# Bias column of the layer norm on Pool, and a reordered gMLP step, in a two-layer hybrid decoder trunk

## The reference, cut to what matters

```python
h = x * (1 + sc) + sh
x = layer_norm(DEEPNORM_ALPHA * x + (1 + gt) * y, g, b)   # y = mixer or MoE of h

z = gelu(h @ w_in + b_in); u, v = split(z)                # the gMLP, u and v of width 2048
v = layer_norm(v, sgu_ln_g, sgu_ln_b)
mixed = einsum('gts,bnsgc->bntgc', tril(w_s), v) + b_s    # over 128 tokens of a chunk, 8 groups
y = (u * mixed) @ w_out + b_out
```

## Time and profile before

| | us |
|---|---|
| median of 3 runs | 2381.33 (2380.76 to 2382.56) |
| the profiled execution, its own time | 2371.53 |
| its span, slowest core (core 3) | 2370.5 |
| spans of the eight cores | 2345.4 to 2370.5 |
| PE busy / DVE / ACT / POOL in the span | 1320.1 / 1281.0 / 618.6 / 447.9 |

### The profile page before, as it was taken

One profiled execution on the slowest core, in us unless ns is written; L12 is line 12 of the kernel. 1 busy time (PEld: TensorE's weight loads), 2 busy tenths in 40 slices (PEclk: granted clock), 3 DMA queues, 4 the chain that ended last, 5 costly groups with the idle time before them and its releaser, 6 DMA issues.

```text
span 2370.5 us, 30701 instructions; the slowest of 8 cores (2345.4 to 2370.5 us)
## 1 busy us (share of the span) xinstructions
PE 1320.1 (56%) x9655; PEld 808.7 (34%) x9655; DVE 1281.0 (54%) x2578; ACT 618.6 (26%) x1191; POOL 447.9 (19%) x562
## 2 busy tenths in 40 slices
PE   1657667675074444553327988888843555556300
PEld 0334334443053333342114444434422433334200
DVE  2465555654354444461338667676644545555488
ACT  1435335342021111121113434434321211112000
POOL 1030020112221111110112221313113111111252
PEclk9778889887587777776668999999976877778655
DMA  9958847489889999999854888668695999999752
GB/s 167 185 115 98 108 73 115 81 97 120 129 157 241 235 220 198 251 217 218 231 123 75 165 160 160 136 140 151 103 192 171 214 255 243 251 258 257 278 197 97
DMA packets 91387, 407.91 MB, mean 172 GB/s; under 512 B 20261, under 2 KB 20261, under 8 KB 79525
## 3 DMA queue, kind: packets, MB, share of 16 engines
q0 software_dynamic: 41584, 211.43, 56.5%
q1 hardware_dynamic: 49626, 194.34, 24.0%
HBM read 449.24 MB, written 160.53 MB: 257 GB/s over the span
## 4 chain that ended last, share of the span: by engine, by line
DMA 34%; PE 23%; DVE 22%; issue 11%; another core or an unknown queue 4%; ACT 3%; POOL 2%; DVEq 1%; SPq 1%; ACTq 0%; POOLq 0%
DMA sb_W<-wb 7%; DMA sb_x<-xd 6%; PE bank L1384 5%; DMA ys<-sb_Z 3%; DMA sb_A<-adaP 3%; DMA sb_W<-ys,sb_idx 3%; PE bank L1076 3%; PE bank L1704 3%; DMA ys<-sb_hT 2%; PE bank L917 2%; DVE sb_x L1450 2%; DMA sb_W<-moe_w 2%; PE bank L1630 2%; DMA xd<-sb_hT 2%
## 5 line engine op out<-in xcount | busy, mean ns | idle before, releaser
L1384 PE MATMUL bank<-sb_hT,sb_W 128*128 128x256 bf16 x1984 | 308.0, 322 | 185.8 <-DMA sb_W<-wb 164.4
L1384 PEld LDWEIGHTS bank<-sb_hT,sb_W 128*128 128x128 bf16 x1984 | 222.2, 115 | 240.8 <-issue 188.3
L1366 ACT ACTIVATE sb_hT<-bank,sb_H 128x256 bf16<-128x256 f32 x256 | 130.1, 561 | 441.5 <-PE bank L1357 433.0
L1371 DVE TENSOR_SCALAR sb_hT<-bank,sb_H 128x256 bf16<-128x256 f32 x256 | 126.8, 537 | 183.3 <-PE bank L1357 147.8
L1409 DVE TENSOR_TENSOR sb_hT<-bank,sb_gtbf 128x512 f32<-128x512 f32 x176 | 121.4, 691 | 76.4 <-DMA ys<-sb_hT 59.8
L1704 PE MATMUL bank<-sb_W,sb_Z 128*128 128x512 bf16 x512 | 137.6, 417 | 14.9 <-ACT sb_Z L1697 14.9
L610 POOL TENSOR_TENSOR sb_rstdt<-sb_mvt,sb_eps_t 128x1 f32<-128x1 f32 x64 | 25.8, 404 | 586.4 <-DVE sb_R L448 247.9
L1630 PE MATMUL bank<-sb_x,sb_Z 128*128 128x512 bf16 x512 | 127.4, 393 | 11.6 <-DVE sb_cact_rep L1685 5.6
L1405 PE MATMUL bank<-sb_W,sb_R 128*128 128x512 bf16 x496 | 130.8, 410 | 1.2 <-DVE sb_hT L1409 1.2
L1661 PE MATMUL bank<-sb_x,sb_Z 128*128 128x512 bf16 x512 | 123.5, 383 | 5.8 <-issue 5.8
L1346 POOL DMA_INDIRECT sb_hT<-xh,sb_slots x64 | 60.9, 951 | 330.6 <-PE bank L1357 286.5
(11 more groups left out here) (260 smaller groups left out, 2696.4 us busy)
## 6 DMA issues: line engine op xcount, KB each, us to landing
wb<-moe_w POOLq DMA_DIRECT2D x38, 1536.0 KB, 16.6
sb_W<-wb SPq DMA_DIRECT2D x36, 1536.0 KB
ys<-sb_hT SPq DMA_DIRECT2D x44, 1024.0 KB
sb_W<-moe_w POOLq DMA_DIRECT2D x26, 1536.0 KB, 21.1
ys<-sb_Z SPq DMA_DIRECT2D x20, 1024.0 KB
sb_A<-adaP POOLq DMA_DIRECT2D x30, 512.0 KB, 14.6
sb_x<-xin SPq DMA_DIRECT2D x16, 512.0 KB, 9.7
xd<-sb_x SPq DMA_DIRECT2D x16, 512.0 KB, 47.0
```

The source lines that it names most:

```text
L1366: S.op("act", (lambda k=k, src=src: lambda e: e.activation(out=hTe[i][:, k, :], in_=src, func=AF.Identity, scale=H1[haff][:, k:k + 1], bia ...
L1371: S.op("dve", (lambda k=k, src=src: lambda e: e.tensor_scalar(out=hTe[i][:, k, :], in0=src, scalar1=H1[haff][:, k:k + 1], scalar2=H0[haff] ...
L1384: S.op("pe", (lambda k=k, f=f, fc=fc: lambda e: e.matmul(banks[bk][:, f * 256:(f + 1) * 256], wgu[:, k, fc:fc + 128], hTe[i][:, k, :], sta ...
```

## The change

1. `ln_stats` now also makes the column -mean x rstd, by two Pool instructions behind `rsqrt` (one multiplies the mean by a constant -1, one multiplies that by rstd), in a column for each tile. The DVE instruction L620 of `ln_xhat` goes.
2. In the gMLP the bn_stats of v leaves `gV` and is issued one step later (`gVs(i+3)`), behind `gU`.
3. The four mean subtractions of a tile are issued one in each step of that tile, ahead of `gB`. bn_aggr and `rsqrt` of v go from cb = 3 of the tile before to cb = 0 of the tile.
4. For the returned tile, `ln_stats`, `ln_xhat` and `finalize_b` go one step later each: from cb = 3, 0, 1 to cb = 0, 1, 2. `tl_combine`, `tl_fetch` and `affine` stay in their steps.

```diff
-        mvt = sb("mvt", [128, NT, 2]); rstdt = sb("rstdt", [128, NT]); nmr_ = [sb(f"nmr{i}", [128, 1]) for i in range(2)]
+        mvt = sb("mvt", [128, NT, 2]); rstdt = sb("rstdt", [128, NT]); nmrt = sb("nmrt", [128, NT])
...
+        S.op("dve", lambda e: e.memset(mone[:], -1.0), writes=[Beps])
...
             rsqrt(rstdt[:, t:t + 1], Brstd_[t], mvt[:, t, 1:2], Bmv_[t])
+            nm = nmrt[:, t:t + 1]
+            S.op("pool", lambda e: e.tensor_tensor(out=nm, in0=mvt[:, t, 0:1], in1=mone[:], op=ALU.mult),
+                 reads=[Bmv_[t], Beps], writes=[Bnmr_[t]])
+            S.op("pool", lambda e: e.tensor_tensor(out=nm, in0=nm, in1=rstdt[:, t:t + 1], op=ALU.mult),
+                 reads=[Brstd_[t], Bnmr_[t]], writes=[Bnmr_[t]])
...
-            S.op("dve", lambda e: e.scalar_tensor_tensor(out=nmr[:], in0=mvt[:, t, 0:1], scalar=-1.0,
-                                                         in1=rstdt[:, t:t + 1], op0=ALU.mult, op1=ALU.mult),
-                 reads=[Bmv_[t], Brstd_[t]], writes=[Bnmr])
-            S.op("act", lambda e: e.activation(out=dst, in_=xa, func=AF.Identity, scale=rstdt[:, t:t + 1], bias=nmr[:]),
-                 reads=[bxa, Brstd_[t], Bnmr], writes=[bdst])
+            S.op("act", lambda e: e.activation(out=dst, in_=xa, func=AF.Identity, scale=rstdt[:, t:t + 1],
+                                               bias=nmrt[:, t:t + 1]),
+                 reads=[bxa, Brstd_[t], Bnmr_[t]], writes=[bdst])
...
             S.op("act", lambda e: e.activation(out=v, in_=banks[bk][:], func=AF.Gelu), reads=[PB[bk]], writes=[bv])
-            S.op("dve", lambda e: e.bn_stats(out=gst[:, i2, cb, :], in_=v), reads=[bv], writes=[Bgst[i2]])
-
-        def v_norm(t, part):
+
+        def gVs(j):
+            t, cb = divmod(j, 4)
             i2 = t % 2
-            if part == 0:
+            S.op("dve", lambda e: e.bn_stats(out=gst[:, i2, cb, :], in_=v32[j % NV]), reads=[Bv32[j % NV]], writes=[Bgst[i2]])
+
+        def v_norm(t, cb):
+            i2 = t % 2
+            if cb == 0:
                 S.op("dve", lambda e: e.bn_aggr(out=mvg[:, i2, :], in_=gst[:, i2, :, :]),
                      reads=[Bgst[i2]], writes=[Bmvg[i2]])
                 rsqrt(rstdg[:, i2:i2 + 1], Brstdg[i2], mvg[:, i2, 1:2], Bmvg[i2])
-            for cb in ((0, 1, 2), (3,))[part]:
...
                 gU(i)
+            if 0 <= i + 3 < 4 * NT:
+                gVs(i + 3)
+            if 0 <= i < 4 * NT:
+                v_norm(t, cb)
             if 1 <= i <= 4 * NT:
                 gB(i - 1)
             if cb == 0 and 0 <= t < NT:
                 ws_scale(t)
-                v_norm(t, 1)
...
-            if cb == 3 and 0 <= t + 1 < NT:
-                v_norm(t + 1, 0)
...
             if cb == 3 and 0 <= t + 3 < NT:
                 tl_combine(t + 3)
-                ln_stats(t + 3)
...
             if 0 <= t + 2 < NT:
                 if cb == 0:
+                    ln_stats(t + 2)
+                if cb == 1:
                     ln_xhat(t + 2, xnb[0], Bxnb[0])
-                if cb == 1:
+                if cb == 2:
                     finalize_b(t + 2, 0, 2, hdst=hTg[(t + 2) % 3], bhdst=BhTg[(t + 2) % 3], on_act=8)
-                if cb == 2:
                     affine(t + 2)
```

More of the change, by code:

```diff
@@ L314, in build @@
         Badfm, BadabT, Bmod = [Buf(f"adfm{j}") for j in range(6)], Buf("adabT"), [Buf(f"mod{i}") for i in range(4)]
-        Bnmr_ = [Buf(f"nmr{i}") for i in range(2)]
+        Bnmr_ = [Buf(f"nmr{t}") for t in range(NT)]; mone = sb("mone", [128, 1])
         fin_i = [0]
@@ L617, in ln_xhat @@
             xa, bxa = xv[t]
-            i = fin_i[0] % 2
-            nmr, Bnmr = nmr_[i], Bnmr_[i]
-            S.op("dve", lambda e: e.scalar_tensor_tensor(out=nmr[:], in0=mvt[:, t, 0:1], scalar=-1.0,
-                                                         in1=rstdt[:, t:t + 1], op0=ALU.mult, op1=ALU.mult),
-                 reads=[Bmv_[t], Brstd_[t]], writes=[Bnmr])
-            S.op("act", lambda e: e.activation(out=dst, in_=xa, func=AF.Identity, scale=rstdt[:, t:t + 1], bias=nmr[:]),
-                 reads=[bxa, Brstd_[t], Bnmr], writes=[bdst])
+            S.op("act", lambda e: e.activation(out=dst, in_=xa, func=AF.Identity, scale=rstdt[:, t:t + 1],
+                                               bias=nmrt[:, t:t + 1]),
+                 reads=[bxa, Brstd_[t], Bnmr_[t]], writes=[bdst])
         def affine(t):
@@ L1627, in gV @@
             bk = next_bank()
-            i2 = t % 2
             for k in range(8):
@@ L1644, in v_norm @@
                 rsqrt(rstdg[:, i2:i2 + 1], Brstdg[i2], mvg[:, i2, 1:2], Bmvg[i2])
-            for cb in ((0, 1, 2), (3,))[part]:
-                q = (4 * t + cb) % NV
-                S.op("dve", (lambda q=q, cb=cb: lambda e: e.scalar_tensor_tensor(
-                    out=vln[cb], in0=v32[q], scalar=mvg[:, i2, 0:1], in1=lng[:, cb * 512:(cb + 1) * 512],
-                    op0=ALU.subtract, op1=ALU.mult))(),
-                     reads=[Bv32[q], Bmvg[i2], Blng], writes=[Bvln[cb]])
+            q = (4 * t + cb) % NV
+            S.op("dve", lambda e: e.scalar_tensor_tensor(
+                out=vln[cb], in0=v32[q], scalar=mvg[:, i2, 0:1], in1=lng[:, cb * 512:(cb + 1) * 512],
+                op0=ALU.subtract, op1=ALU.mult),
+                 reads=[Bv32[q], Bmvg[i2], Blng], writes=[Bvln[cb]])
         def ws_scale(t):
```

## The result

The changed kernel takes 2352.12 us in the median of 4 runs (2344.96 to 2368.08), against 2381.05 of 4 runs before: ratio 0.9886, 95% interval 0.9849 to 0.9922, which is 19 to 36 us less. A repeat on another chip gave 0.9891 (0.9849 to 0.9933).

What follows compares the result with a forecast made beforehand. PE sets the pace in the steady gMLP, its repeating waits all ending with DVE. Terms +6 (attention) -19 (steady) +0 -8 (start) -12 (drain) +4 (crowding) +1 (tail) = -28 us, from 2381.3 to 2353; range 2341 to 2366, with rivals 2334 to 2377.

Steps and rivals of the forecast that it cites:

- the steady gMLP: Steady gMLP: matrix waits -14, clock -4, bank waits -5, waits before gC +4, together -19 us (-9 to -30).
- the drain: End of the gMLP: the column on Pool is ready sooner and ln_xhat waits less, -12 us (-3 to -27).
- crowding: Steady gMLP: DMA share rises from 0.75 to 0.79, sums wait more often for their tile, +4 us (0 to 15).
- The wait in front of gC: Steady gMLP: one subtraction now also precedes the product with u, 0.7 us more on each of six waits, +4.
- the waits only move: Rival, chance 0.07: the subtraction ahead of the product and attention's longer path eat the matrix gain; 2381 us, within 4.
- covers Pool: Steady gMLP: one subtraction and two products (0.7 + 1.06 us) on DVE cover Pool's making of rstd of v.
- The returned tile comes too late: Rival, chance 0.07: DVE is held more than 6 us, transposes stop PE in every tile; 2398 us.
- DMA engines take it back: Rival, chance 0.15: the residual slot's 29 us stay longer than the tile, so sums and matrix wait; 2375 us.
- The attention phase: Attention: two Pool instructions delay ACT by 0.4 us in each of 16 tiles, +6 us (0 to +17).
- DVE then waits for ACT, so it wins nothing: Attention: DVE's 1.06 us wait for Pool goes, but waiting for ACT replaces it, so no gain.
- The start: Start of the gMLP: first PE wait covered, 3 us gone ahead of the second, -8 us (0 to -13).
- the store goes out ahead of those loads: Drain: with the column some 8 us sooner, ln_xhat's store precedes the first experts' loads; part of the -12 us.

Runs made afterwards that it cites:

- the pair without conversions: Changed kernel and kernel before, each without the 24 bf16 weight conversions beside the gMLP: 1.0145 and 1.0294 of before; gMLP 589.3 and 618.3 us.
- the value part: Value statistics and subtractions moved; run as the changed kernel with the returned tile's statistics, normalization and transposes in their old steps: 1.0064 of before.

## Why the prediction was right, and where its terms were not

The time came out as predicted (2352 against 2353), and its mechanism, DVE's order in the gMLP, is what the runs show. That the sum came within 1 us is luck: the steady gMLP and the drain gave 6 and 10 us less than I had, attention some 9 more, and MoE 0, which I had at nothing, is longer by an amount that single profiles don't fix.

*The steady gMLP* (−19, with +4 of crowding): measured −9. In the stretch of 1300 to 1722 us, from which I forecast, the wait for the matrix fell by 12 us on core 3 and by 16 in the mean of the cores (22.9 to 7.1), against the 14 forecast, so this term was right. The bank waits went as forecast (6.3 to 0). The 4 us for the clock did not come: the granted clock of the stretch went from 0.94 to 0.93 in the mean. And PE got a wait that no term of the sum has by name, in gB for the gelu of u, 2.0 to 25.2 us a core. *The wait in front of gC*, which I had longer by 0.7 us in each tile, went to gB, where it is as long as before (20.4 and 21.0). Here, and only here, the rival "the waits only move" was right. The step "bn_stats and now one subtraction precede the product" was sound for DVE but missed that PE's gB, ahead of gC, needs that same subtraction.

*Which part pays.* I credited the removal of three subtractions from the stretch ahead of the matrix (2.1 us) as much as the returned tile's `ln_stats` (1.4). The runs give all of it to the returned tile. The sentence that failed is that DVE's work "covers Pool": without the returned tile's step Pool makes rstd of v behind four column instructions and two gathers, and DVE waits 44.0 us a core. It holds only because the other part of the change clears the column instructions out of Pool's queue. "The returned tile comes too late" did not happen: PE doesn't wait at its transposes on any core from 1300 to 1722 us. I counted what each step costs on DVE and didn't list what stands ahead of rstd on Pool.

*Crowding* (+4): 10 to 12 by the pair without conversions, near the upper end of 15 that I gave, with the spread said there. DVE's waits for the tile rose by 17 us a core. I read the base from core 3, whose DMA share of 0.75 was the lowest of the eight (0.82 in the mean), and took the share to grow with the bytes, to 0.79; it grew to 0.92 there (0.90 in the mean) for some 3% more bytes. "DMA engines take it back" was the rival nearest to the truth in this phase.

*The attention phase* (+6): its last `ln_xhat` is 5.4 us earlier in the mean of the kernels (565.7 against 571.1), −3 at its end. The delay on ACT was 0.18 us, not the 0.4 that I took: 0.59 us from the end of rstd to ACT's start in this tile, against 0.41 in the earlier trace rows. Timeline:

```profile
193.50 0.56 POOL L618 TENSOR_TENSOR sb_rstdt<-sb_rstdt,sb_mhalf 128x1 f32<-128x1 f32 x1
194.04 0.18 POOL L610 TENSOR_TENSOR sb_nmrt<-sb_mvt,sb_mone 128x1 f32<-128x1 f32 x1
194.36 0.19 POOL L612 TENSOR_TENSOR sb_nmrt<-sb_nmrt,sb_rstdt 128x1 f32<-128x1 f32 x1
...
194.65 1.24 ACT L624 ACTIVATE sb_hT<-sb_x,sb_nmrt,sb_rstdt 128x1024 bf16<-128x1024 f32 x1 [9.49 <-POOL sb_nmrt L612]
```

What failed is the step "DVE then waits for ACT, so it wins nothing": PE waits for DVE's normalization 54.7 us a core from 170 to 570 us, and 48.7 with the column on Pool, so DVE is on the path too.

*The start* (−8): −10. Of PE's waits in the earlier trace rows, the 7.20 us for the matrix is gone and the 5.39 at the transposes too (1225 to 1310 us before, L648 45.4 us in 2; after, L650 40.4 in 2, of which 40.1 is the longest in both). On core 3 gB now waits 7.7 us there for the gelu of u, the subtraction and the product, which I hadn't counted. The mechanism is the one named, but the runs give the start to all three parts together, the column among them. *The drain* (−12): −2. The column is there in time, as forecast, but each `ln_xhat` now waits for the store of the one before, and that store takes 30 us as before (from 1699.03 to ACT's start at 1729.22; from 1719.98 to 1750.04 in the earlier trace rows):

```profile
1729.22 1.24 ACT L624 ACTIVATE sb_xnb<-sb_hT,sb_nmrt,sb_rstdt 128x1024 bf16<-128x1024 f32 x1 [10.43 <-DMA xh<-sb_xnb]
...
1759.17 1.24 ACT L624 ACTIVATE sb_xnb<-sb_hT,sb_nmrt,sb_rstdt 128x1024 bf16<-128x1024 f32 x1 [22.49 <-DMA xh<-sb_xnb]
```

Against the earlier trace rows, 17.33 and 11.79 us of waiting became 10.43 and 22.49, so "ACT not held before the second last `ln_xhat`" failed, and what the one tile wins the last one loses: the bound was the store, not the column. The step that failed is "the store goes out ahead of those loads". The store and the first load of expert weights behind it in SP's queue, before and then after:

```profile
1719.98 0.32 SPq L374 DMA_DIRECT2D xh<-sb_xnb  x1
...
1722.54 0.92 SPq L374 DMA_DIRECT2D sb_x<-wb  x2
```

```profile
1699.03 0.32 SPq L374 DMA_DIRECT2D xh<-sb_xnb  x1
...
1702.09 0.97 SPq L374 DMA_DIRECT2D sb_x<-wb  x2
```

Both came out some 20 us sooner, so the loads still follow the store by 3 us.

*MoE 1* (0): 413.0 and 416.6 against 414.3, as forecast. *The tail* (+1): 128.7 and 128.0 against 128.4. Two more Pool instructions for each tile change nothing. The second one takes 1.14 us there against 0.19 in attention (all of the tail on Pool, core 3: busy us, mean ns | idle before):

```profile
L612 POOL TENSOR_TENSOR sb_nmrt<-sb_nmrt,sb_rstdt 128x1 f32<-128x1 f32 x16 | 18.2, 1137 | 2.3
```

By the rule of the Trainium skill ("SBUF — State Buffer", "Who interferes with whom") a Pool instruction that reads SBUF and a DVE instruction with two SBUF inputs exclude each other. Pool loses here again, as in the earlier trace rows; that DVE loses is not seen in the phase's length.

## What to carry to other kernels

When work moves to a later step, list what then stands ahead of each small instruction on every queue, Pool's gathers among them: with the value part of this change and the returned tile in its old steps the kernel was 0.6% slower than before with two gathers ahead of one column on Pool, and as fast as before (0.9986, 0.9958 to 1.0013) with them behind it. Test the parts of a change on their own in both surroundings; here one part carries the gain and the other, which cost 29 us of gMLP without it, is only rendered harmless. Take the base of a forecast from all cores: core 3 had the lowest DMA share and 16.1 us of a wait whose mean was 22.9. A wait behind a burst on an in-order engine belongs to the burst: changing which instruction comes first behind it moved these 20 us twice, from gC to gB and back, and never shortened them.

## What was not expected of the hardware

A store of 512 KB took up to 24 us beside weight conversions of 1.5 MB, and issuing the same conversions in pairs in other steps made the waits for the loads longer (44 against 30 us a core), not shorter: the stores took less time and the loads more than that longer. The busy share of the DMA engines is no measure of the bytes: from 0.82 to 0.90 in the mean of the cores for some 3% more of them. Phases of unchanged code differed by up to 9 us (MoE 0, 524 to 533) between profiled executions, in the mean over eight cores, part of it between chips, and the same kernel by 0.9% between chips (2352 and 2373 us).
